# Second layer norm: the last down-projection piece in thirds of 430, 344 and 258 columns instead of three of 344

## What is computed

```python
def _layer_norm(x, g, b):
    mu = jnp.mean(xf, axis=-1, keepdims=True)
    var = jnp.mean(jnp.square(xf - mu), axis=-1, keepdims=True)
    return (xf - mu) * lax.rsqrt(var + LN_EPS) * g + b

def _conv_ffn(h, prev, w_up, w_conv, b_conv, w_down):     # D_FF = 2816 = 22 tiles of 128
    ...
    return (jax.nn.gelu(a_c + b_conv) * gate) @ w_down, buf_new

f, ffn_new = _conv_ffn(h, ffn_prev, w_up, w_ffn_conv, b_ffn_conv, w_down)
y = _layer_norm(DEEPNORM_ALPHA * h + f, ln2_g, ln2_b)       # D_MODEL = 1024 = 8 tiles of 128
```

## Time and profile before

| | |
|---|---|
| median of 3 runs | 1712.01 us (1710.29 to 1712.67) |
| profiled execution | 1714.81 us |
| its span | 1713.0 us |
| PE busy | 1679.5 us, 98% |
| DVE (VectorE) busy | 938.2 us, 55% |
| ACT (ScalarE) busy | 586.7 us, 34% |
| POOL (GpSimd) busy | 495.7 us, 29% |
| last piece: start of slice 0 | 1620.44 us |

### The profile page before, as it was taken

One profiled execution on the slowest core, in us unless ns is written; L12 is line 12 of the kernel. 1 busy time (PEld: TensorE's weight loads), 2 busy tenths in 40 slices (PEclk: granted clock), 3 DMA queues, 4 the chain that ended last, 5 costly groups with the idle time before them and its releaser, 6 DMA issues.

```text
span 1713.0 us, 35073 instructions
## 1 busy us (share of the span) xinstructions
PE 1679.5 (98%) x13959; PEld 1630.8 (95%) x13959; DVE 938.2 (55%) x1619; ACT 586.7 (34%) x1195; POOL 495.7 (29%) x287
## 2 busy tenths in 40 slices
PE   8999999999999999999999999999999999999997
PEld 7999999999989888889999999999999999999996
DVE  2003337778456677751664689766666666211157
ACT  3124333444432545631432462322222233301123
POOL 2121111111111112111432333555444443614320
PEclk9999999999999999998999999999999999999998
DMA  4110115455562344324671034444444416431202
GB/s 187 49 49 32 42 48 177 119 130 124 164 196 91 122 151 131 110 72 156 238 263 59 26 136 153 154 153 153 167 164 154 164 74 262 158 116 51 79 7 96
DMA packets 134576, 213.22 MB, mean 124 GB/s; under 512 B 60032, under 2 KB 100160, under 8 KB 132672
## 3 DMA queue, kind: packets, MB, share of 16 engines
q1 hardware_dynamic: 133472, 209.89, 36.5%
q10 hardware_dynamic: 1008, 1.98, 0.4%
HBM read 159.29 MB, written 79.95 MB: 140 GB/s over the span
## 4 chain that ended last, share of the span: by engine, by line
PE 93%; DVE 3%; ACT 1%; DMA 1%; issue 1%; POOL 1%; ACTq 0%; SPq 0%; DVEq 0%; POOLq 0%
PE U L965 35%; PE B L1436 15%; PE U L1070 11%; PE U L1436 6%; PE U L1357 5%; PE U L1502 3%; PE B L965 3%; PE B L1056 2%; PE B L1031 1%; PE B L1048 1%; PE B L1216 1%; PE B L1248 1%; PE B L1286 1%; PE U L1477 1%; PE B L1039 1%
## 5 line engine op out<-in xcount | busy, mean ns | idle before, releaser
L845 POOL TENSOR_TENSOR wl<-stage,wh 128x1024 fp32r<-128x1024 f32 x81 | 195.3, 2411 | 751.5 <-ACT wh L1519 738.5
L965 PE MATMUL U<-xh,wh 128*128 128x344 f32 x960 | 313.2, 326 | 0.2 <-ACT qkv L1523 0.2
L965 PE MATMUL U<-xl,wh 128*128 128x344 f32 x960 | 306.7, 319 | 0.0
L965 PE MATMUL U<-xh,wl 128*128 128x344 f32 x960 | 306.6, 319 | 0.0
L965 PEld LDWEIGHTS U<-xh,wh 128*128 128x128 f32 x960 | 180.5, 188 | 0.6 <-ACT qkv L1523 0.5
L965 PEld LDWEIGHTS U<-xh,wl 128*128 128x128 f32 x960 | 180.6, 188 | 0.0
L965 PEld LDWEIGHTS U<-xl,wh 128*128 128x128 f32 x960 | 180.4, 188 | 0.0
L1519 ACT ACTIVATE wh<-stage 128x1024 fp32r<-128x1024 f32 x77 | 81.1, 1053 | 140.3 <-PE U L965 112.8
L1070 PE MATMUL U<-xh,wh 128*128 128x344 f32 x384 | 126.9, 330 | 0.0
L1070 PE MATMUL U<-xl,wh 128*128 128x344 f32 x384 | 126.6, 330 | 0.0
L1070 PE MATMUL U<-xh,wl 128*128 128x344 f32 x384 | 126.1, 328 | 0.0
(11 more groups left out here) (448 smaller groups left out, 4452.8 us busy)
## 6 DMA issues: line engine op xcount, KB each, us to landing
stage<-in_wu SPq DMA_DIRECT2D x126, 512.0 KB, 3.7
out_shift<-in_cache SPq DMA_DIRECT2D x16, 1022.0 KB
hid_scr<-cc SPq DMA_DIRECT2D x22, 516.0 KB, 2.9
gate_scr<-gth SPq DMA_DIRECT2D x16, 516.0 KB, 3.1
gates<-gate_scr SPq DMA_DIRECT2D x8, 1032.0 KB, 5.9
dn_scr<-thb SPq DMA_DIRECT2D x12, 512.0 KB, 2.8
tok_scr<-pre SPq DMA_DIRECT2D x48, 128.0 KB, 3.8
qkv<-in_cache SPq DMA_DIRECT2D x10, 512.0 KB, 6.1
```

What stands on the lines that cost most here:

```text
L845: nc.gpsimd.tensor_tensor(wl[:, par, :], stage[:, par, :], wh[:, par, :].bitcast(F32), ALU.subtract).then_inc(w_lo, 1)
L965: ins = nc.tensor.matmul(dst, a[:, par, w], b[:, xk, third(j)], start=first and n == 0 and m == 0, stop=last and n == len(ks) - 1 and m == 2)
```

## The change

The thirds of the last piece and of the second norm get cuts of their own: 0, 430, 774 and 1032, that is five, four and three spots of 86 tokens. Everything of the last piece is cut by them: PE's slices, evictions, squares, sums, statistics, the mean's and the root's spreads, subtractions, scalings, affines and stores. The first norm keeps its equal thirds through the same functions. The squares of the last piece get a buffer of their own, `last_sq`, since three of 430 columns don't fit in `ab`. The columns of the statistics in PSUM and in `lst` are spaced for five spots. Third 1's work is moved: its spread from slice 19 to slice 20, its pairs 0, 1, 2 from steps 19, 20, 21 to 20, 21, 22, its affines from 20, 21, 22 to 21, 22, 23.

```diff
+NORM_CUTS = ((0, TW, 2 * TW, TOK), (0, 5 * SPOT, 9 * SPOT, TOK))
+SPOTS_MOST = 5
+def norm_part(ln, j):
+    return slice(NORM_CUTS[ln][j], NORM_CUTS[ln][j + 1])
+def norm_width(ln, j):
+    return NORM_CUTS[ln][j + 1] - NORM_CUTS[ln][j]
+def norm_spots(ln, j):
+    return norm_width(ln, j) // SPOT
...
-            lst = held(late, "lst", [P, THIRDS, 12])
+            lst = held(late, "lst", [P, THIRDS, 3 * SPOTS_MOST])
+            last_sq = held(part, "last_sq", [P, THIRDS, SPOTS_MOST * SPOT])
...
-        LAST_PAIRS = {13: ((0, 0),), 14: ((0, 1),), 16: ((0, 2), (0, 3)), 19: ((1, 0),), 20: ((1, 1),), 21: ((1, 2),)}
-        LAST_AFFINE = {14: ((0, 0),), 15: ((0, 1),), 17: ((0, 2), (0, 3)), 20: ((1, 0),), 21: ((1, 1),), 22: ((1, 2),)}
+        LAST_PAIRS = {13: ((0, 0),), 14: ((0, 1),), 16: ((0, 2), (0, 3)), 20: ((1, 0),), 21: ((1, 1),), 22: ((1, 2),)}
+        LAST_AFFINE = {14: ((0, 0),), 15: ((0, 1),), 17: ((0, 2), (0, 3)), 21: ((1, 0),), 22: ((1, 1),), 23: ((1, 2),)}
...
+        def squares_of(ln, j, s):
+            return ab[:, s % 3 * TW:(s % 3 + 1) * TW] if ln == 0 else last_sq[:, s % 3, 0:norm_width(1, j)]
...
-                    sp.dma_start(O["y"][:, two(q), third(j)], acc[:, two(q), third(j)]).then_inc(y_stored, 16)
+                    sp.dma_start(O["y"][:, two(q), norm_part(1, j)], acc[:, two(q), norm_part(1, j)]).then_inc(y_stored, 16)
...
-                    if k == 2 and s in (10, 13, 17, 19):
-                        {10: ln_stats, 13: ln_spread, 17: ln_stats, 19: ln_spread}[s](1, s // 16)
+                    if k == 2 and s in (10, 13, 17, 20):
+                        {10: ln_stats, 13: ln_spread, 17: ln_stats, 20: ln_spread}[s](1, s // 16)
-                        ins = nc.tensor.matmul(U[:, s % 3, 0:TW], a[:, c], b[:, k, third(j)], start=k == 0 and m == 0,
+                        ins = nc.tensor.matmul(U[:, s % 3, 0:norm_width(1, j)], a[:, c], b[:, k, norm_part(1, j)], start=k == 0 and m == 0,
...
-                nc.vector.tensor_tensor(a, a, U[:, s % 3, 0:TW], ALU.add).then_inc(used, 1)
+                nc.vector.tensor_tensor(a, a, U[:, s % 3, 0:norm_width(1, j)], ALU.add).then_inc(used, 1)
```

More of the change, by code:

```diff
@@ L885, in root @@
                 pool.wait_ge(ln_var, ln * THIRDS + j + 1)
-                nc.gpsimd.tensor_tensor(lst[0:SPOT, j, 8:12], lst[0:SPOT, j, 4:8], mhalf[0:SPOT, 0:SPOTS], ALU.pow).then_inc(
+                n = norm_spots(ln, j)
+                nc.gpsimd.tensor_tensor(lst[0:SPOT, j, 2 * n:3 * n], lst[0:SPOT, j, n:2 * n], mhalf[0:SPOT, 0:n], ALU.pow).then_inc(
                     ln_root, 1)
@@ L1325, in ln_stats @@
                 for n, src in enumerate((total, power)):
-                    for w in range(SPOTS):
-                        a, c = j * TW + w * SPOT, 8 * j + n * SPOTS + w
+                    for w in range(norm_spots(ln, j)):
+                        a, c = NORM_CUTS[ln][j] + w * SPOT, 2 * SPOTS_MOST * j + n * norm_spots(ln, j) + w
                         ins = nc.tensor.matmul(B7[0:SPOT, c:c + 1], src[:, a:a + SPOT], cst[:, C_INV:C_INV + 1],
@@ L1332, in ln_stats @@
                     pe.wait_ge(ln_cent, LN_CENTRED[ln])
-                nc.tensor.matmul(spread[j][0][:, 0:TW], inv[:], total[:, third(j)], start=True, stop=True).then_inc(ln_mean, 1)
+                nc.tensor.matmul(spread[j][0][:, 0:norm_width(ln, j)], inv[:], total[:, norm_part(ln, j)], start=True,
+                                 stop=True).then_inc(ln_mean, 1)
             def ln_spread(ln, j):
                 pe.wait_ge(ln_root, ln * THIRDS + j + 1)
-                for w in range(SPOTS):
+                n = 2 * norm_spots(ln, j)
+                for w in range(norm_spots(ln, j)):
                     ins = nc.tensor.matmul(spread[j][1][:, w * SPOT:(w + 1) * SPOT],
-                                           lst[0:SPOT, j, 8 + w:9 + w].to_broadcast([SPOT, P]), ident[0:SPOT, 0:SPOT],
+                                           lst[0:SPOT, j, n + w:n + w + 1].to_broadcast([SPOT, P]), ident[0:SPOT, 0:SPOT],
                                            start=True, stop=True)
@@ L1808, in _, with square @@
                 merge_high(f)
-            def square(f, j, s, count):
+            def square(ln, f, j, s, count):
                 act.wait_ge(used, count)
-                dst = power[:, third(j)] if f == 0 else ab[:, s % 3 * TW:(s % 3 + 1) * TW]
-                nc.scalar.activation(dst, acc[:, f, third(j)], ACT.Square).then_inc(ln_sq, 1)
+                c = norm_part(ln, j)
+                dst = power[:, c] if f == 0 else squares_of(ln, j, s)
+                nc.scalar.activation(dst, acc[:, f, c], ACT.Square).then_inc(ln_sq, 1)
             def affine(ln, j, q):
@@ L1819, in affine @@
                     g, b = (C_G1, C_B1) if ln == 0 else (C_G2, C_B2)
-                    ins = nc.scalar.activation(acc[:, f, third(j)], acc[:, f, third(j)], ACT.Identity,
+                    ins = nc.scalar.activation(acc[:, f, norm_part(ln, j)], acc[:, f, norm_part(ln, j)], ACT.Identity,
                                                bias=cst[:, b + f:b + f + 1], scale=cst[:, g + f:g + f + 1])
@@ L1846, in _ @@
                     ffn_high(s - 17)
-                square(f, j, s, MIX_USED + s + 1)
+                square(0, f, j, s, MIX_USED + s + 1)
                 for pair in MIX_AFFINE.get(s, ()):
@@ L1966, in _ @@
                 n = s if f < 4 else max(s, SUMMED[s - 3] + 1)
-                square(f, j, s, LAST_USED - 3 * KT + n + 1)
+                square(1, f, j, s, LAST_USED - 3 * KT + n + 1)
                 for pair in LAST_AFFINE.get(s, ()):
@@ L2435, in _, with ln_sums @@
             spread = LN_BANKS
-            def ln_sums(f, j, s, count, squares):
+            def ln_sums(ln, f, j, s, count, squares):
                 if f == 0:
@@ L2441, in ln_sums @@
                 dve.wait_ge(used, count)
-                a, t, p = acc[:, f, third(j)], total[:, third(j)], power[:, third(j)]
-                ls.link(nc.vector.tensor_tensor(t, acc[:, 0, third(j)] if f == 1 else t, a, ALU.add))
+                c = norm_part(ln, j)
+                a, t, p = acc[:, f, c], total[:, c], power[:, c]
+                ls.link(nc.vector.tensor_tensor(t, acc[:, 0, c] if f == 1 else t, a, ALU.add))
                 dve.wait_ge(ln_sq, squares)
-                ins = nc.vector.tensor_tensor(p, p, ab[:, s % 3 * TW:(s % 3 + 1) * TW], ALU.add)
+                ins = nc.vector.tensor_tensor(p, p, squares_of(ln, j, s), ALU.add)
                 if f == KT - 1:
@@ L2453, in ln_moments @@
                 dve.wait_ge(ln_stat, ln * THIRDS + j + 1)
-                mean, var, scratch = lst[0:SPOT, j, 0:4], lst[0:SPOT, j, 4:8], lst[0:SPOT, j, 8:12]
-                ls.link(nc.vector.tensor_copy(lst[0:SPOT, j, 0:8], B7[0:SPOT, 8 * j:8 * j + 8]))
+                n, c = norm_spots(ln, j), 2 * SPOTS_MOST * j
+                mean, var, scratch = lst[0:SPOT, j, 0:n], lst[0:SPOT, j, n:2 * n], lst[0:SPOT, j, 2 * n:3 * n]
+                ls.link(nc.vector.tensor_copy(lst[0:SPOT, j, 0:2 * n], B7[0:SPOT, c:c + 2 * n]))
                 ls.link(nc.vector.tensor_tensor(scratch, mean, mean, ALU.mult))
@@ L2459, in spread_of @@
             def spread_of(ln, j, n):
-                return spread[j][n][:, 0:TW].unsqueeze(1).to_broadcast([P, 2, TW])
+                return spread[j][n][:, 0:norm_width(ln, j)].unsqueeze(1).to_broadcast([P, 2, norm_width(ln, j)])
             def ln_shift(ln, j, q):
                 dve.wait_ge(ln_mean, ln * THIRDS + j + 1)
-                a = acc[:, two(q), third(j)]
+                a = acc[:, two(q), norm_part(ln, j)]
                 ls.link(nc.vector.tensor_tensor(a, a, spread_of(ln, j, 0), ALU.subtract))
@@ L2487, in _ @@
                 nc.vector.scalar_tensor_tensor(a, a, ALPHA, U[:, s % 3, 0:TW], ALU.mult, ALU.add).then_inc(used, 1)
-                ln_sums(f, j, s, MIX_USED + s + 1, s + 1)
+                ln_sums(0, f, j, s, MIX_USED + s + 1, s + 1)
                 for pair in MIX_PAIRS.get(s, ()):
@@ L2712, in _ @@
                 dve.wait_ge(slice_done, 3 * U_LAST + s + 1)
-                a = acc[:, f, third(j)]
+                a = acc[:, f, norm_part(1, j)]
                 if s in (10, 17):
                     ln_moments(1, s // 16)
-                nc.vector.tensor_tensor(a, a, U[:, s % 3, 0:TW], ALU.add).then_inc(used, 1)
+                nc.vector.tensor_tensor(a, a, U[:, s % 3, 0:norm_width(1, j)], ALU.add).then_inc(used, 1)
                 for n in LAST_SUMS.get(s, (s - 1,) if s > 5 else ()):
-                    ln_sums(n % KT, n // KT, n, LAST_USED - 3 * KT + n + 1, THIRDS * KT + n + 1)
+                    ln_sums(1, n % KT, n // KT, n, LAST_USED - 3 * KT + n + 1, THIRDS * KT + n + 1)
                 for pair in LAST_PAIRS.get(s, ()):
```

## The result

The changed kernel takes 1718.22 us (median of 11 runs, 1716.15 to 1719.86), the kernel before 1712.85 us (11 runs, the three shown above among them). The ratio is 1.0021, 95% interval 1.0012 to 1.0029: slower by 2.1 to 5.0 us. The medians lie further apart, 5.4 us; the ratio, 3.6 us, is what I go by. A second set, five rounds on another occasion, gave 1.0028 (1.0019 to 1.0038). The forecast of 1713.5 us and its range (to 1716.2) lay too low.

What follows compares the result with a forecast made beforehand. PE was taken to bound the kernel, busy 98% of the span, with VectorE limiting from slice 19. +3.90 us to the last sum and -2.43 in the tail gave +1.47, so 1713.5 us; range with rivals 1710.4 to 1716.2.

Steps and rivals of the forecast that it cites:

- The three stages with different limits: Last piece: PE limits to slice 19, VectorE from there to the last sum, then a serial tail of 15.97 us.
- The 430-column pitch: Third 0's multiplies: 0.1947 us each by extending a line from narrower widths, so a slice takes 3.50 us.
- The bubble ahead of slice 1: Slice 1's wait for the first low half on POOL, claimed hidden by a longer slice 0: -0.30 us.
- The wait at third 1's statistics: Slice 17: PE stalls 1.49 us for VectorE's second sum of slice 15, where there was no wait before.
- The last sum: VectorE's last sum ends 11.14 us after slice 20's eviction, at 1700.93 instead of 1697.03: +3.90 us.
- The tail: Serial work after the last sum, now 258 wide: 2.43 us shorter, about 13.5 us in place of 15.97.
- the narrow stores: Last store in the tail, 258 KB for 344 at 2.4 us: no gain taken, at most -0.6 us.
- VectorE's narrow operations in slices 20 to 23: Eleven counted; if time were proportional to width they would take 0.4 us less than the forecast counts.
- the price of the stall in slice 17: Stall of 1.49 us ahead of third 1's statistics, with the clock expected at 1.00 behind it.
- the rival that did: Slice 17's stall makes TensorE's clock fall, costing 5 us (nearly nothing to 7.1): 1718.5 us; 8 in 100.
- The move to slices 20 to 22: Third 1's spread and centring moved from slice 19 to 20: claimed to add no wait.
- The base: Median before the change, 1712.01 us, to which the forecast difference was added; spread of runs +-1.2.

Runs made afterwards that it cites:

- x4: Changed kernel with third 1's spread and three pairs back at slices 19, 20, 21; ratio to the kernel before 1.0012.
- x3: Changed kernel with third 1's statistics and their moments moved from slice 17 to 18; ratio to the kernel before 1.0002.
- x6: Changed kernel with third 0's spread and first two pairs in 12 and 13, third 1's spread and pairs back in 19 to 21; ratio 1.0008.
- x7: Uneven thirds in their best order plus 30 dummy multiplies of 258 columns behind the last slice; ratio to the kernel before 0.9998.
- x2: Changed kernel with twelve dummy multiplies of 258 columns ahead of the statistics in slice 17; ratio to the kernel before 1.0020.
- x8: Kernel before, equal thirds, with 15 dummy multiplies of 344 columns behind the last slice; ratio to the kernel before 0.9995.
- x9: Kernel before with third 1's spread in slice 18, pairs in 18 to 20, and 10 dummy multiplies behind the last slice; 1712.67 us, ratio 0.9987.
- x5: Kernel before, equal thirds, with only the change's buffers (15-column lst, squares in last_sq); ratio to the kernel before 1.0006.
- x10: Changed kernel, unedited, profiled once more; the clock fell, last piece 96.0 us.
- x1: Changed kernel, unedited, timed again in five rounds beside the kernel before; ratio 1.0028, last piece 94.4 us.
- x11: Changed kernel, unedited, profiled once more; the clock did not fall, last piece 94.4 us.

## Why the prediction was wrong

**Right, to a few tenths.** The three stages with different limits. The 430-column pitch: from the first multiply of slice 0 to that of slice 1 it is 3.52 us for 18, forecast 3.50. The bubble ahead of slice 1 is gone. The wait at third 1's statistics: 1.47 us over the pitch, forecast 1.49. The last sum 11.17 us after slice 20's eviction, forecast 11.14. The tail 13.4 us, forecast 13.54. Without a fall of the clock the last piece is 1.9 us longer, forecast 1.5: the missing 0.4 is 0.3 in third 0 (slice 13 evicted 49.10 us after the start, forecast 48.82) and 0.2 in the sums behind the wait, 1.39 us where 1.15 was put, less 0.1 in the tail. There the narrow stores, put at no gain, took 2.2 us (median of four) in place of 2.4. One count of the prediction is wrong without touching the sum: VectorE's narrow operations in slices 20 to 23 are fourteen and not eleven, so the time that a cost by width alone would save is 0.5 us and not 0.4.

**The step that failed** is the price of the stall in slice 17. The sum put nothing on the clock behind it, and the rival that did had 8 in 100, because one row of before showed 1.00 after a gap of 1.58 us. One gap of one execution is no evidence that the clock holds. In five profiles with the same 1.3 us wait in slice 17 (four of the changed kernel, and x4) the clock fell behind it twice. And the gap of the earlier trace rows itself, which lies far ahead of the change and is 1.45 to 1.91 us long in all fourteen profiles, was followed by a fall once, in x3:
```profile
1441.22 0.61 PE L1500 MATMUL U<-xh,wh 128*128 128x344 f32 x1 [1.91 <-DVE gq L2645]
```
```profile
1442.00:1443.00 1.00, 1.00 (x5) 1.00 (x4) 1.00 (x2) 0.77 (x1) 0.00 (x0) 0.50 1.03 405
```
The prediction also let the length of the gap decide. By itself it does not: 1.3 us was followed by a fall, and a gap of 3.0 us near 1092 us (x6, x7) was not. The rival's size was wrong too, 5 us where the pairs of profiles show 1.5, since the clock came back after some 3.4 us and did not stay down over three slices. That its time, 1718.5 us, lies beside the measured median, 1718.22, is chance: the last piece lost 1.5 us by the clock and not 5.

**The move to slices 20 to 22** was called free of new waits, which is so; but the prediction's own row of VectorE's idle time ahead of slice 19 was not used to price it. It costs 0.9 us (x4). That sum was in the forecast, so it misled no number, only the reading of what the uneven thirds are worth.

**The base.** The median before was 1712.01 from three runs and 1712.85 from eleven: 0.8 us of the miss. The range allowed 1.2 for this and nothing for a fall.

**What stays open.** The last piece explains 1.9 to 3.4 us, and the two ratios say 3.6 and 4.8. Of the 4.7 us between the forecast and the median, 0.8 is the base, 0.4 the small terms above and at most 1.5 the fall of the clock; about 2 us have no cause here. The time of x2 and of x4 to x8 lies 0.9 to 1.7 us above what their last piece shows too, that of x9 0.5, that of x3 not at all. All but x6, which is just outside, are within their intervals, and runs that share their comparison runs also share those runs' chance, so this may be nothing; and it is no mark of the uneven thirds, since x5 and x8 have equal ones. x5 tried the buffers and could not tell.

The last piece starts at 1619.3 to 1623.6 us in nine profiles with uneven thirds, mean 1621.4, and at 1619.6 to 1621.0 in five with equal thirds, mean 1620.4. Part of that is again the clock, far ahead of the change: near 1092 us PE has a gap of 2.6 to 3.0 us in all fourteen profiles, and in nine of them it was granted 0.50 for some 3.4 us behind it. The five without that fall are the five that start earliest. Among them uneven (three) and equal thirds (two) start alike, at 1619.9 and 1619.8 on average; among the nine with it at 1622.1 (six) and 1620.8 (three). Whether something ahead of the last piece is slower in the changed kernel by about 1 us, and what, was not settled.

## What to carry to other kernels

When the last part of a pipeline is made smaller, the work of the part before it falls on shorter slices: the follower engine's queue, at a fixed order, then has less time for the same operations, and what the short tail gives back is lost ahead of it. Count the follower's step against the leader's slice at the seam before cutting, and move its work into its idle steps first. A wait put into a stream of multiplies costs its length and, in some executions, the clock behind it, so one profile without a fall does not clear it. If the leader is idle ahead of a tail anyway, filling that idle time was worth more in the last piece here (1.8 us, x8) than the smaller tail, of whose 2.6 us only 0.4 were left in its best order (x6).

## What the runs showed of the hardware

- The same gap of 1.3 us in PE's stream, in the same program, led to 0.50 of the clock for 3.4 us in two profiles and to none in two others; the fall began 2.2 to 2.4 us after PE was busy again (after, x10).
- The length of a gap alone did not decide: the gap of 2.6 to 3.0 us near 1092 us was followed by a fall in nine of fourteen profiles, with 2.62 us in x3 and not with 3.00 in x6; the one of 1.45 to 1.91 us near 1440 us once (x3).
- A fall behind the wait cost 1.5 us: 54 multiplies of 258 columns in 7.95 and 7.99 us (after, x10), 6.43 and 6.42 without one (x1, x11).
- The mean granted clock of an execution goes with its time: of the 35 runs of the kernel before beside x5 to x8, the seven at 0.993 took 1711.4 us on average, the eleven at 0.990 1716.6.
- Behind the last slice, 2.8 to 4.9 us of idle PE left the clock at 0.50 for the tail. With dummy multiplies in it the clock stayed at 1.00 through one-column sums and the mean (x7, x8).
- Sixteen sum records right behind a wait took 1.39 us (x1), behind a busy stretch 1.15 (x3); x2, with dummies ahead, 1.23.
